# Moving five small jobs of a mixer stage from VectorE to ScalarE

## The reference, cut to what matters

```python
proj = a @ w_in                      # a = rmsnorm(h); 1024 -> attention q,k,v | 1536 delta columns | z | a,b
# (A) attention over a window of 128 keys, 8 heads
s = q k^T * 64**-0.5 - slope * dist          # masked outside the band
m = max(max(s), sink); e = exp(s - m)
probs = e / (sum(e) + exp(sink - m))         # the probability scaling
att = probs @ v
# (B) gated DeltaNet, 8 heads of 64
qkv = silu(sum_j x[t-3+j] * w[j], j = 0..3)  # causal convolution with 4 taps
G = cumsum(g)
decay = exp(G_i - G_j) for i >= j            # the decay arguments are min(G_i - G_j, 0)
M = I + strict(beta k k^T * decay);  X = solve(M, [beta v, beta k exp(G)])
o = q exp(G) S + (q k^T * decay) v_new;  S = S exp(g_last) + k_tail^T v_new
h = h + concat(att, rmsnorm(o) * silu(z)) @ w_out
```

## Time and profile before

| | |
|---|---|
| time, three executions | 4484.65, 4494.29, 4495.69 us (median 4494.29) |
| time of the profiled execution | 4486.98 us |
| its span, first to last instruction | 4485.2 us |
| mean granted TensorE clock | 0.849 of full speed |
| busy, share of the span | PE 75%, DVE 69%, POOL 40%, ACT 21% |
| mixer (tiles 0 to 8) | from 0 to about 2150 us |

### The profile page before, as it was taken

The page is one execution under the profiler, slowest core; times in us unless marked ns, Lnnn a source line. Parts: engine busy times, 40 slices in busy tenths (PEclk is TensorE's granted clock), DMA queues, the critical chain, the costliest instruction groups (busy, mean ns, idle before and its releaser), DMA issues.

```text
span 4485.2 us, 45523 instructions
## 1 busy us (share of the span) xinstructions
PE 3377.5 (75%) x15950; PEld 2722.8 (61%) x15950; DVE 3098.2 (69%) x6931; ACT 961.2 (21%) x2156; POOL 1814.8 (40%) x1503
## 2 busy tenths in 40 slices
PE   3657978676765676556566899898996999889954
PEld 2537977676765675555465677676774566556621
DVE  0234486979698869886698688688786645772486
ACT  0102212111111112011596133132340010000022
POOL 4000003333234633455233555555455545662464
PEclk8658988888877787778666999999998999999977
DMA  9323427666666876778577999999999988997786
GB/s 298 87 76 131 170 109 267 229 260 228 241 225 254 309 295 212 257 284 305 219 262 283 369 388 398 336 395 373 356 352 377 372 304 341 397 398 271 272 301 221
DMA packets 434399, 1258.25 MB, mean 281 GB/s; under 512 B 62039, under 2 KB 179319, under 8 KB 406506
## 3 DMA queue, kind: packets, MB, share of 16 engines
q0 software_dynamic: 209232, 762.41, 45.7%
q1 hardware_dynamic: 210554, 421.53, 26.3%
q10 hardware_dynamic: 14384, 71.40, 4.0%
HBM read 1194.11 MB, written 86.15 MB: 285 GB/s over the span
## 4 chain that ended last, share of the span: by engine, by line
PE 22%; DMA 15%; DVE 6%; ACT 4%; POOL 2%; issue 1%; ACTq 1%; SPq 1%; DVEq 1%; POOLq 0%
PE pbank L1988 17%; DMA v_blocks<-in_peer_v_dram 9%; DMA expert_rows<-in_peer_u_dram,slot_data 5%; ACT late_sb L2102 2%; POOL expert_rows L333 2%; DVE late_sb L2244 2%; PE pbank L2015 2%; PE pbank L1956 2%; PE pbank L1973 2%; DVE expert_rows L395 1%; ACT late_sb L2104 1%; ACTq L2103 1%; DMA expert_rows<-in_peer_v_dram,slot_data 1%; SPq L1880 0%; DVE late_sb L2256 0%
## 5 line engine op out<-in xcount | busy, mean ns | idle before, releaser
L333 POOL DMA_INDIRECT expert_rows<-in_peer_u_dram,slot_data x1088 | 1380.1, 1268 | 2299.7 <-DVE slot_data L395 1441.7
L395 DVE CUSTOM_DVE_ANT_0 expert_rows<-expert_rows,c_three 128x1024 f32<-128x1024 f32 x1088 | 1296.7, 1223 | 338.9 <-DMA expert_rows<-in_peer_u_dram,slot_data 325.5
L1988 PE MATMUL pbank<-v_blocks,w_chunks 128*128 128x512 f32 x3072 | 1395.7, 612 | 145.5 <-DMA v_blocks<-in_peer_v_dram 88.1
L1988 PEld LDWEIGHTS pbank<-v_blocks,w_chunks 128*128 128x128 f32 x3072 | 941.6, 310 | 547.2 <-issue 180.0
L333 POOL DMA_INDIRECT expert_rows<-in_peer_v_dram,slot_data x320 | 382.4, 1195 | 295.1 <-DVE late_sb L2244 230.7
L2244 DVE SCALAR_TENSOR_TENSOR late_sb<-expert_rows,slot_data,late_sb 128x1024 f32<-128x1024 f32 x320 | 411.4, 1286 | 121.8 <-DMA expert_rows<-in_peer_v_dram,slot_data 109.8
L1973 PE MATMUL pbank<-late_sb 128*128 128x128 f32 x1536 | 273.3, 338 | 86.9 <-ACT late_sb L2104 59.5
L1973 PEld LDWEIGHTS pbank<-late_sb 128*128 128x128 f32 x1536 | 250.6, 244 | 133.4 <-issue 123.1
L1076 PE MATMUL mbank<-att_sc,att_pT 128*128 128x128 f32 (+1 forms) x672 | 137.9, 390 | 236.8 <-DVE att_sc L1670 213.3
L1076 PEld LDWEIGHTS mbank<-att_sc,att_pT 128*128 128x128 f32 (+1 forms) x672 | 128.3, 295 | 244.0 <-issue 218.2
L2256 DVE TENSOR_SCALAR late_sb<-iota,slot_rows 128x128 f32<-128x128 f32 x768 | 219.5, 372 | 70.4 <-ACT slot_rows L2093 53.9
(11 more groups left out here) (381 smaller groups left out, 4201.8 us busy)
## 6 DMA issues: line engine op xcount, KB each, us to landing
w_ring<-relaid_weights SPq DMA_DIRECT2D x168, 1024.0 KB, 6.8
v_blocks<-in_peer_v_dram SPq DMA_DIRECT2D x256, 512.0 KB, 11.0
w_chunks<-spread_weights SPq DMA_DIRECT2D x64, 768.0 KB, 20.7
spread_weights<-weight_stage ACTq DMA_DIRECT2D x12, 2048.0 KB, 10.3
spread_weights<-late_sb ACTq DMA_DIRECT2D x12, 2048.0 KB, 10.7
late_sb<-relaid_weights ACTq DMA_DIRECT2D x20, 1024.0 KB, 8.5
expert_rows<-in_peer_u_dram,slot_data POOLq DMA_INDIRECT x1088, 8.2
w_ring<-in_w_in_dram SPq DMA_DIRECT2D x9, 1024.0 KB, 12.2
```

What stands on the lines that cost most here:

```text
L333: nc.gpsimd.indirect_dma_start(rows[:, n % RING, :], None, u_tab if kind == "u" else v_tab, bass.IndirectOffsetOnAxis(ap=idx[:, at:at + 1] ...
L395: nc.vector.tensor_tensor_reduce(out=rows[:, n % RING, :], in0=rows[:, n % RING, :], in1=c[:, i % 3, :], scale=1.0, scalar=0.0, op0=ALU.mu ...
L1988: m = t_.matmul(bank[2 * i + b][:, :], wc[:, k % 3, i * P:(i + 1) * P, r], vb[:, n % 4, b * 512:(b + 1) * 512], start=(e == 0), stop=(e == ...
```

## The change

Five kinds of work go from VectorE to ScalarE. In prompt tiles and, except for the probabilities and the convolution, in tile 0:

1. decay arguments: eight DVE instructions (line 1575) become eight ACT instructions `Relu(g - x)`, 128 columns each, and the exponential after them takes scale -1;
2. probability scaling: one DVE instruction over 2048 columns (line 1585) becomes eight ACT instructions of 256 columns, behind the decay exponential;
3. row copies: all five are done by ACT, the semaphore `rT_v` is gone;
4. the input's eviction `x_T`: two DVE instructions of 512 columns become eight ACT instructions of 128 columns with the weight as a per-partition scale;
5. the convolution's last tap: ACT writes it into `cacc` straight from PSUM, four more instructions in each `conv_in`;
With 5, VectorE's convolution keeps taps 0 to 2, all as multiply-and-add.

```diff
-                        pe.wait_ge(s["e_in"], i + 1)
+                        pe.wait_ge(s["exp_ready"], i + 1)
...
                     pe.wait_ge(s["rT_a"], i + 1)
-                    pe.wait_ge(s["rT_v"], i + 1)
...  (ACT)
+                def x_T(i, r):
+                    act.wait_ge(s["xT_ps"], i + 1)
+                    for k in range(KD):
+                        m = ac.activation(aT[:, k, 0:r], bank[6 + k // 4][:, (k % 4) * P:(k % 4) * P + r], ACT.Copy, scale=g_mix[:, k:k + 1])
+                    m.then_inc(s["aT_ready"], 1)
...  (ACT, conv_in)
+                        src = bank[6 + b % 2][:, :].rearrange("p (c t) -> p c t", c=4)
+                        ac.activation(cin[:, b * 4:b * 4 + 4, 3:3 + P], src, ACT.Copy)
+                        for c in range(4):
+                            m = ac.activation(cacc[:, b * 4 + c, :], src[:, c, :], ACT.Copy, scale=cw[:, TAPS - 1, b * 4 + c:b * 4 + c + 1])
...  (ACT, tile)
                     act.wait_ge(s["e_in"], i + 1)
+                    for hh in range(DH):
+                        ac.activation(dt_[0:r, hh, 0:r], bank[hh // 4][0:r, (hh % 4) * P:(hh % 4) * P + r], ACT.Relu,
+                                      scale=-1.0, bias=gt[0:r, 6, hh:hh + 1])
...
-                    ac.activation(dt_[0:r, :, 0:r], dt_[0:r, :, 0:r], ACT.Exp).then_inc(s["exp_ready"], 1)
+                    act.drain()
+                    ac.activation(dt_[0:r, :, 0:r], dt_[0:r, :, 0:r], ACT.Exp, scale=-1.0).then_inc(s["exp_ready"], 1)
                     if not sampled:
+                        act.wait_ge(s["prob_sum"], i)
+                        for hh in range(AH):
+                            m = ac.activation(sc[:, hh, :], sc[:, hh, :], ACT.Copy, scale=am[:, 0, hh:hh + 1])
+                        m.then_inc(s["probs_ready"], 1)
...
-                    for n, b in ((1, 4), (2, 5), (4, 0)):
+                    for n, b in ((1, 4), (2, 5), (0, 6), (3, 7), (4, 0)):
...  (ACT, level n == 1)
+                        if ahead and n == 1:
+                            x_T(i + 1, P)
...  (DVE)
-                    for hh in range(DH):
-                        m = v.tensor_scalar(dt_[0:r, hh, 0:r], bank[hh // 4][0:r, (hh % 4) * P:(hh % 4) * P + r],
-                                            gt[0:r, 6, hh:hh + 1], 0.0, ALU.subtract, ALU.min)
...
-                        v.reciprocal(am[:, 0, :], am[:, 5, :])
-                        dve.drain()
-                        v.tensor_tensor(sc[:, :, :], sc[:, :, :], bc(am[:, 0, :], 2 * WIN), ALU.mult).then_inc(s["probs_ready"], 1)
+                        v.reciprocal(am[:, 0, :], am[:, 5, :]).then_inc(s["prob_sum"], 1)
...
-                    dve.wait_ge(s["rT_ps"], 2 * i + 1)
-                    for n, b in ((0, 6), (3, 7)):
-                        m = v.tensor_copy(rT[:, n, :, 0:r], bank[b][:, :].rearrange("p (c t) -> p c t", c=4)[:, :, 0:r])
-                    m.then_inc(s["rT_v"], 1)
+                    dve.drain()
...
-                            if ahead and n == 1:
-                                x_T(i + 1, P)
...
                             if ahead and n == 4:
                                 conv(i + 1, False, 0, (0, 1, 2))
                             if ahead and n == 5:
-                                conv(i + 1, False, 0, (3,))
                                 conv(i + 1, False, 1, (0, 1))
...
-                            conv(i + 1, False, 1, (2, 3))
+                            conv(i + 1, False, 1, (2,))
...
-                        conv(i + 1, False, 2, (2, 3))
+                        conv(i + 1, False, 2, (2,))
```

More of the change, by code:

```diff
@@ L583, in mixer_half @@
                      "cin_ready kv_sb q_sb z_sb silu_done conv_done rows_ps sq_done ssq_done rn_sqrt "
-                     "soft_in soft_out gate_ready gsum_ps e_in exp_ready drow_ready rT_ps rT_a rT_v gram_ps "
+                     "soft_in soft_out gate_ready gsum_ps e_in exp_ready drow_ready rT_ps rT_a gram_ps "
                      "kgs_ps y0_ready b_ready t_ps t_sb zz_ps xx_ready y1_ps y1_sb ty_ps ty_sb yz_ps vn_ready "
                      "o_ps upd_ps osq_done ossq orms dn_ready dnT_ps dnT_sb score_ps sc_ready nm_ready "
-                     "prob_done probs_ready pT_ps pT_sb att_ps att_sb h_ready h_out "
+                     "prob_done prob_sum probs_ready pT_ps pT_sb att_ps att_sb h_ready h_out "
                      "state_out stc_in stc_ps stc_sb cache_in state_in vnew_in kcT_ps kcT_sb over_clear "
@@ L1268, in conv_in @@
                     else:
-                        m = ac.activation(cin[:, b * 4:b * 4 + 4, 3:3 + P],
-                                          bank[6 + b % 2][:, :].rearrange("p (c t) -> p c t", c=4), ACT.Copy)
+                        src = bank[6 + b % 2][:, :].rearrange("p (c t) -> p c t", c=4)
+                        ac.activation(cin[:, b * 4:b * 4 + 4, 3:3 + P], src, ACT.Copy)
+                        for c in range(4):
+                            m = ac.activation(cacc[:, b * 4 + c, :], src[:, c, :], ACT.Copy, scale=cw[:, TAPS - 1, b * 4 + c:b * 4 + c + 1])
                     m.then_inc(s["cin_ready"], 1)
@@ L1301, in front @@
                     x_rms(i, r)
+                    x_T(i, r)
                     if sampled:
@@ L1471, in x_norm, with n_taps @@
                     v.tensor_scalar(xn[0:r, :], x[0:r, :], st[0:r, 2:3], None, ALU.mult).then_inc(s["xn_ready"], 1)
[L1473 to L1479, removed]
+                def n_taps(sampled):
+                    return TAPS if sampled else TAPS - 1
                 def conv(i, sampled, b, taps):
@@ L1491, in conv @@
                                 src, dst = cin[:, c, j:j + P], cacc[:, c, :]
-                            if j == 0:
+                            if sampled and j == 0:
                                 m = v.tensor_scalar(dst, src, cw[:, j, c:c + 1], None, ALU.mult)
@@ L1495, in conv @@
                                 m = v.scalar_tensor_tensor(dst, src, cw[:, j, c:c + 1], dst, ALU.mult, ALU.add)
-                        if j < TAPS - 1:
+                        if j < n_taps(sampled) - 1:
                             dve.drain()
-                    if b == 2 and taps[-1] == TAPS - 1:
+                    if b == 2 and taps[-1] == n_taps(sampled) - 1:
                         m.then_inc(s["conv_done"], 1)
@@ L1506, in front @@
                     x_norm(i, r)
-                    x_T(i, r)
                     if sampled:
@@ L1510, in front @@
                     for b in range(3):
-                        conv(i, sampled, b, range(TAPS))
+                        conv(i, sampled, b, range(n_taps(sampled)))
                 def residual(i, r, n):
@@ L1568, in tile @@
                         if sampled:
-                            v.tensor_copy(egb[c * HD:(c + 1) * HD, :, :],
+                            m = v.tensor_copy(egb[c * HD:(c + 1) * HD, :, :],
                                           bank[7][c * HD:(c + 1) * HD, 64:128].rearrange("p (b h e) -> p b h e", b=DB, e=2)[:, :, :, c])
                         else:
-                            v.tensor_copy(eg[c * HD:(c + 1) * HD, :],
+                            m = v.tensor_copy(eg[c * HD:(c + 1) * HD, :],
                                           bank[7][c * HD:(c + 1) * HD, 64:64 + DH].rearrange("p (h e) -> p h e", e=2)[:, :, c])
-                    for hh in range(DH):
-                        m = v.tensor_scalar(dt_[0:r, hh, 0:r], bank[hh // 4][0:r, (hh % 4) * P:(hh % 4) * P + r],
-                                            gt[0:r, 6, hh:hh + 1], 0.0, ALU.subtract, ALU.min)
                     m.then_inc(s["e_in"], 1)
```

## The result

| | before | after |
|---|---|---|
| median of the runs | 4494.99 us (8 runs) | 4457.4 us (8 runs) |
| time of the profiled execution | 4486.98 us | 4460.57 us |
| span | 4485.2 us | 4458.6 us |
| mean granted TensorE clock | 0.849 | 0.849 |

The ratio of the times is 0.9906, 95% interval 0.9878 to 0.9933. That is a gain of 42 us (30 to 55); the medians alone give 37.6. The forecast was 4466 with an own range of 4452 to 4480, a gain of 25.

A forecast was written before the change was run, and what follows sets the result against it. Bound: a relay of VectorE and PE in each mixer tile. 11.9 - 2.8 + 5.2 + 3 + 9 = 26.3, less about 1 for tile 0, gives 25 us; between 4462 and 4469 it took 4466, own range 4452 to 4480.

The forecast's parts named there:

- The relay: In each mixer tile VectorE mostly sets the pace, PE sometimes; saved VectorE work counts only up to the next meeting point.
- new waits at named places: Waits: line 1591 for ScalarE, second residual for PE, line 1624 3 us or more, line 1631 about 1.5 us.
- Part 1: Decays and probability scaling, up to second residual: 11.9 us gained in tiles 2 to 8, 2.8 lost in tile 1.
- the rival in which the clock falls: Closer packing of PE's work lowers its clock; a mean lower by 0.05 costs 34 us, giving 4500; chance 0.05.
- PE's last output products end at 1024.84: Tile 4: they hold the second residual to 1024.9, though it could start at 1023.5; gain 2.8 us.
- The prediction's bound for tile 1: Tile 1's loss at the probability transposes, taken as 2.8 us, has bounds 0.7 (transposes at the fast clock) and 4.
- cover: Tile 4: scaling ends at 1023.6, PE's transposes wait until 1025.5 anyway, so ScalarE has 1.9 us to spare.
- Part 2: Row copies, up to the Gram matrices: 2.2 us in tiles 6 and 8, 0.8 in tile 2, together 5.2.
- Part 3: Input's eviction, before line 1631 level 2: nothing in tiles 1, 3, 4, 5; 1.0 each in 2, 6, 7; 3 us.
- Part 4: Convolution's last tap: net 1.5 us per tile where VectorE sets the pace, 9 us in all.
- all of VectorE's time counts: PE's chains are themselves held by VectorE: 10.5 us per full tile, about 65 over tiles 2 to 8, 4428; chance 0.07.
- the gain is taken back by a table load: No change: late gathers take half the gain (4482), or Relu after Exp loads tables (4488); chance of both 0.22.

The follow-up runs named there:

- part 1 alone: Kernel before with only the decay arguments and probability scaling moved to ScalarE: 4482.2 us, ratio 0.9968.
- parts 2, 3 and 4: Three kernels, each the kernel before with one move to ScalarE: row copies 4491.53 us, input's eviction 4487.14 us, convolution's last tap 4483.7 us.

## Why the prediction was right, and short by 12 us

**The relay.** Right. It was to be shown by new waits at named places, and three of four have the size that was written down; the fourth was 1.9 for 3. The wait at line 1682 stayed (27.1 to 28.1).

**Part 1.** The mechanism was right and the term was too small: 11.9 - 2.8 = 9.1 us predicted, 14 (7 to 22) measured for this part alone, and 17.9 up to the Gram matrices in its own trace. Tiles 3 to 8 gained 23.8 us up to the Gram matrices instead of 16.3, and tile 1 lost less. Three sizes were off.
- The 16 transposes were priced at the same duration before and after. The prediction had both durations in front of it, and the wait that goes with each, but used them only for the rival in which the clock falls. In tiles 3, 4, 5 and 7 they became 5.8 us shorter together. This is a term that the prediction put at nothing, and 5.8 of the 9.7 us that it lacked up to the Gram matrices.
- "PE's last output products end at 1024.84" was taken as fixed. In the changed kernel they end 0.8 us earlier in tile 4, counted from the end of the score step (17.5 instead of 18.2): the first of their eight groups took 1.89 us instead of 2.51, again the clock (1.00 granted in it, 0.73 before). Added over tiles 3 to 7 the transposes start 2.8 us earlier than predicted (1.0, 0.8, -0.6, 1.1 and 0.6).
- Tile 1 lost 0.5 us, not 2.8. PE did begin the probability transposes later there, behind ScalarE's chain: 7.6 us, of which 3.8 were brought along from ahead. But they now run straight into the transposes of the rows, which wait for nobody, and these took 1.91 us instead of 3.67:

```profile
409.29 3.34 PE L1017 MATMUL mbank<-ident,att_sc 128*128 128x128 f32 x16 [12.11 <-ACT att_sc L1365]
...
412.47 1.91 PE L1024 MATMUL mbank<-ident,dn_rows 128*128 128x128 f32 x16
```

Before, PE stood idle between the two and did the second at the lower clock:

```profile
406.90 3.67 PE L1024 MATMUL mbank<-ident,dn_rows 128*128 128x128 f32 x16 [1.55 <-DVE dn_vb L1605]
```

The prediction's bound for tile 1, 0.7 "at the fast clock", is near the measured 0.5, but partly by luck: the transposes it meant, those of line 1017, stayed slow (3.34 us), and the ones behind them became fast.

The scaling cost nothing in tile 4, as said, with 1.5 us of cover left for the 1.9 predicted; done twice, it costs 1.9 there and 3.4 in tile 3.

**Part 2.** 5.2 predicted, 6 (-2 to 13) measured, which by itself shows nothing; the timeline of this part alone has the places and about the sizes (0.9, 2.1 and 1.6 in tiles 2, 6 and 8, none in tile 4). In the full change VectorE in tiles 6 and 8 still comes to the Gram matrices without a wait, as it had to for the gain to count there. Tile 8 got 1.3 and not 2.2.

**Part 3.** 3 predicted, 7 (-2 to 15) measured: not against it, but no proof either. That nothing is gained at this place in tile 4 is shown: line 1636 at level 2 waits 1.51 us, 1.28 more than before, which is the whole eviction; with the eviction moved alone, line 1631 waits 1.64.

**Part 4.** 9 predicted, 8 (1 to 15) measured. (The 9 has 1.1 for tile 2, where its own text has 0.4; by the text it would be 8.3.) With part 3 it makes the second half of the tiles, 12 predicted and 15.6 read, but with a scatter from tile to tile (-3.0 to 5.5) that the prediction did not have, and as large as the terms themselves; the trace of part 1 alone, in which these halves are unchanged, reads -8.4 in them. So the agreement of the sums here may be luck. A likely source of the scatter is that other dot products meet late gathers; no run shows it.

**The rivals.** That all of VectorE's time counts (65 us as written; 10.5 in each of seven tiles, less what tile 8 doesn't have, is nearer 70) is out: 38 were gained (55 at most by the interval), and of these some 8 by the clock and not by VectorE at all. That the gain is taken back by a table load is out: there is none. The waits for gathers are 8 us longer (109 for 102), less than that rival had (half the gain); and they seem to come from part 1: up to the end of the mixer its trace has 108 us of them and that of the scaling done twice 111, those of parts 2, 3 and 4 have 98, 96 and 105. With one trace of each this isn't proven. The lower clock did not come: the mean is 0.849 in both profiles, in the prompt tiles it went from 0.82 to 0.83, and at line 1017 it rose. This rival had its sign the wrong way round, and the prediction had named the reason against it itself (shorter idle ahead of PE's work) without giving that a price.

**Left open.** The clock accounts for about 8 of the surplus (the table's 6.1 and 1.8 of the row transposes in tile 1). The rest of the tiles' account (+5 in the tiles, -3 in tile 0) lies within the scatter from tile to tile, and the runs don't separate it; nor do they show by their times whether parts 2 and 3 are worth anything alone, or in which tiles part 4 gains. Every trace is of one execution. A further split of the feed was not tried.

## What to carry to other kernels

Walk from one meeting point to the next and ask at each who is second: that gave the places and, up to the Gram matrices and but for one effect, about the sizes. The effect: if an edit ends a wait of several microseconds ahead of a block of TensorE work, look in the trace how long the same block takes after a short wait, and add the difference: here 1.6 us, on top of some 3 us of wait. And look for the largest waits that an edit leaves alone; here a table of shares moved work into one of them and brought 52 us, more than the five edits together.

## What the runs showed of the hardware

- The 16 transposes of line 1017 took 1.94 to 1.97 us behind every idle time from 0.8 to 1.9 us. Behind 2.5 us and more (up to 17.5) they took 3.15 to 3.68 us in all but four cases: 2.91 behind 3.22, 2.54 behind 3.03, 2.99 behind 2.48 and 1.97 behind 2.90. That is from nine kernels with eight prompt tiles each. The idle time just ahead doesn't settle it alone: 2.90 us left them fast in one kernel, 2.65 and 2.74 made them slow in two others (3.47 and 3.51 us).
- Prices on ScalarE in fp32 with a per-partition operand, overlapped: 0.27 us for 128 columns (`Relu` from PSUM, 2.15 for eight), 0.41 us for 256 columns (3.28 for eight). The same work took VectorE 2.16 and 2.29 us. (The Trainium skill, page "ScalarE: Activation LUTs", section "Rules for kernel authors", would leave both on VectorE as the faster per element. For the decays the two engines are equal here, for the scaling ScalarE is slower by 1 us, and the move pays nonetheless, as long as the cover lasts.)
- `Relu` and `Copy` right behind `Exp` brought no table load in any prompt tile.
